# Expert weights of a mixture of experts: small load units for the first four experts, whole up matrices for the others, and the last down projection split by output columns

## What is computed

```
gate = one group of 4, top 2 of its 8 experts      # gate (n, 32), mostly zero
for e in range(32):                                # D_MODEL 1024, D_EXPERT 256
    hu = xt @ w_up[e]                              # (n,1024) @ (1024,512)
    h  = silu(hu[:, :256]) * hu[:, 256:]
    y += gate[:, e:e+1] * (h @ w_down[e])          # (n,256) @ (256,1024)
out = layernorm(ALPHA * x + y)
```

## Time and profile before

| | |
|---|---|
| time, median of 3 runs | 657.33 us (656.35 to 657.81) |
| the profiled execution | 656.87 us, its span 654.7 us |
| TensorE matmuls busy | 574.6 us, 88% of the span |
| VectorE, ScalarE, GpSimd busy | 297.1, 91.5, 42.8 us |
| moved by DMA | 163.51 MB, mean 250 GB/s |
| chain that ended last | TensorE 65%, VectorE 16%, DMA 15% |

### The profile page before, as it was taken

One profiled execution on the slowest core, in us unless ns is written; L12 is line 12 of the kernel. 1 busy time (PEld: TensorE's weight loads), 2 busy tenths in 40 slices (PEclk: granted clock), 3 DMA queues, 4 the chain that ended last, 5 costly groups with the idle time before them and its releaser, 6 DMA issues.

```text
span 654.7 us, 8625 instructions
## 1 busy us (share of the span) xinstructions
PE 574.6 (88%) x3514; PEld 362.4 (55%) x3514; DVE 297.1 (45%) x794; ACT 91.5 (14%) x215; POOL 42.8 (7%) x54
## 2 busy tenths in 40 slices
PE   6999999869999979999789996999999869778481
PEld 4556656556588757777566654875563424422130
DVE  1355675596765789788473386311001100100007
ACT  1001211014001232223100211011111101000010
POOL 0000000000100143223000000000000000000000
PEclk9999999995999989999899997799999979797896
DMA  8963044561244457564268645699999999999941
GB/s 301 374 247 128 2 162 187 184 195 49 67 128 132 125 182 235 139 218 140 88 257 343 231 209 226 239 394 407 419 366 419 420 419 419 421 418 420 420 189 68
DMA packets 47132, 163.51 MB, mean 250 GB/s; under 512 B 5842, under 2 KB 22700, under 8 KB 34420
## 3 DMA queue, kind: packets, MB, share of 16 engines
q1 hardware_dynamic: 38272, 138.78, 55.0%
q0 software_dynamic: 3472, 14.31, 6.4%
q10 hardware_dynamic: 5348, 9.86, 4.2%
HBM read 160.14 MB, written 2.77 MB: 249 GB/s over the span
## 4 chain that ended last, share of the span: by engine, by line
PE 65%; DVE 16%; DMA 15%; issue 2%; SPq 1%; ACT 0%; DVEq 0%
DMA ring<-in_w_up 13%; PE bank L665 12%; PE bank L494 10%; PE bank L939 6%; PE bank L456 4%; PE bank L926 4%; PE bank L784 4%; PE bank L908 4%; PE bank L1006 3%; PE bank L974 2%; PE bank L848 2%; PE bank L829 2%; PE bank L535 2%; PE bank L761 2%; DVE proj L1389 2%
## 5 line engine op out<-in xcount | busy, mean ns | idle before, releaser
L665 PE MATMUL bank<-work,ring 128*128 128x264 f32 x384 | 93.7, 397 | 0.0
L494 PE MATMUL bank<-ring,work 128*128 128x512 f32 (+2 forms) x224 | 90.5, 546 | 0.6 <-DMA ring<-in_w_in 0.6
L939 PE MATMUL bank<-ring,work 128*32 128x512 f32 x384 | 67.2, 672 | 19.6 <-DMA ring<-in_w_up 13.2
L665 PEld LDWEIGHTS bank<-work,ring 128*128 128x128 f32 x384 | 71.8, 193 | 16.0 <-issue 4.8
L494 PEld LDWEIGHTS bank<-ring,work 128*128 128x128 f32 x224 | 40.2, 190 | 31.0 <-issue 27.0
L2023 DVE SCALAR_TENSOR_TENSOR work<-work,bank 128x256 f32<-128x256 f32 x8 | 3.4, 422 | 100.9 <-ACT work L1276 100.9
L939 PEld LDWEIGHTS bank<-ring,work 128*32 128x32 f32 x384 | 18.4, 122 | 52.9 <-issue 52.8
L939 PE MATMUL bank<-proj,work 128*32 128x512 f32 x128 | 35.0, 697 | 10.4 <-DMA ring<-in_w_up 10.4
L926 PE MATMUL bank<-gates 128*128 128x256 f32 x144 | 36.6, 411 | 0.0
L2036 DVE COPY gates<-bank 128x512 f32<-128x512 f32 x8 | 5.5, 692 | 66.3 <-PE bank L1006 66.3
L926 PEld LDWEIGHTS bank<-gates 128*128 128x128 f32 x144 | 34.8, 335 | 0.5 <-issue 0.4
(11 more groups left out here) (305 smaller groups left out, 766.5 us busy)
## 6 DMA issues: line engine op xcount, KB each, us to landing
ring<-in_w_up SPq DMA_DIRECT2D x24, 2048.0 KB, 18.8
ring<-in_w_down SPq DMA_DIRECT2D x12, 2048.0 KB, 27.9
ring<-in_w_in SPq DMA_DIRECT2D x22, 1024.0 KB, 5.4
proj<-in_w_up SPq DMA_DIRECT2D x8, 2048.0 KB, 24.1
proj<-in_w_down SPq DMA_DIRECT2D x4, 2048.0 KB, 27.9
ring<-in_w_o SPq DMA_DIRECT2D x4, 1024.0 KB, 8.1
ring<-in_cache_mem_k ACTq DMA_DIRECT2D x1, 2048.0 KB, 7.8
ring<-in_cache_mem_v ACTq DMA_DIRECT2D x1, 2048.0 KB, 14.0
```

Of the source, the lines that this page charges most:

```text
L494: last = mm(bank[2 * (i % 2 if i < MEMC else 0) + t][:, 0:w], lhs[:, k, 128 * t:128 * t + 128], rhs[:, k % 4, :], start=(k == 0), stop=(k ...
L665: last = mm(b[:, 0:TOK], w[:, k, 128 * (n % 2):128 * (n % 2) + 128], xT[:, k, 0:TOK], start=(k == 0), stop=(k == KT - 1))
L939: last = mm(bank[5][32 * j:32 * j + 32, :], xTe[q // 2 % 2][:, k, s0:s0 + CAP], w2[j // 2][:, j % 2, r, :], start=(k == 0), stop=(k == KT ...
```

## The change

Quad 0 gets small units: an up unit holds rows k = 2u and 2u + 1 of all four experts (runs of 4 KB), a down unit one of the two rows f of all four (4 KB). TensorE takes them one at a time (`first_up`), between the gathers, and frees each when it is done.

Quads 1 to 7 get whole up matrices: an up unit is one expert, a run of 16 KB a partition. `up_rows` waits for expert j's unit at k = 0 and frees all four at k = 7. Down units are as before, apart from the first and the last quad.

The down units of the last quad hold all four experts for one half `dh` of the output columns (runs of 2 KB, two DMAs a unit). `down(7)` runs one half of the columns, frees its unit, then the other; ScalarE's copy waits only for the first. `combine_last(dh)` takes each half by itself, and VectorE's statistics are split in the same way (`y_part`). The same instructions are run as before, in another order.

```diff
             def expert_unit(w, u, e0):
-                d = wslot[w].rearrange("p (j n) -> p j n", j=2)
-                e = e0 + 2 * (u % 2)
                 if u < UPS:
-                    s = w_up[bass.ds(e, 2), :, :].rearrange("j (p r) n -> p j (r n)", p=128)
-                    at = 2048 * (u // 2)
+                    sp.dma_start(wslot[w], w_up[bass.ds(e0 + u, 1), :, :].rearrange("j (p r) n -> p (j r n)", p=128))\
+                        .then_inc(quad_in[w], 16)
                 else:
-                    s = w_dn[bass.ds(e, 2), :, :].rearrange("j (p r) n -> p j (r n)", p=128)
-                    at = 0
-                sp.dma_start(d, s[:, :, at:at + 2048]).then_inc(quad_in[w], 16)
+                    sp.dma_start(wslot[w].rearrange("p (j n) -> p j n", j=2),
+                                 w_dn[bass.ds(e0 + 2 * (u - UPS), 2), :, :].rearrange("j (p r) n -> p j (r n)", p=128))\
+                        .then_inc(quad_in[w], 16)
+            def row_unit(w, u):
+                d = wslot[w].rearrange("p (j n) -> p j n", j=4)
+                if u < UPS:
+                    s = w_up[0:4, :, :].rearrange("j (p r) n -> p j (r n)", p=128)
+                    at = 1024 * u
+                else:
+                    s = w_dn[0:4, :, :].rearrange("j (p r) n -> p j (r n)", p=128)
+                    at = 1024 * (u - UPS)
+                sp.dma_start(d, s[:, :, at:at + 1024]).then_inc(quad_in[w], 16)
+            def column_unit(w, dh):
+                d = wslot[w].rearrange("p (r j n) -> p r j n", r=2, j=4)
+                s = w_dn[NE - 4:NE, :, :].rearrange("j (p r) n -> p r j n", p=128)
+                for r in range(2):
+                    sp.dma_start(d[:, r, :, :], s[:, r, :, 512 * dh:512 * dh + 512]).then_inc(quad_in[w], 16)
...
-                expert_unit(w, n % WPQ, 4 * (n // WPQ))
+                if n < WPQ:
+                    row_unit(w, n)
+                elif n >= QUADS * WPQ - 2:
+                    column_unit(w, n - QUADS * WPQ + 2)
+                else:
+                    expert_unit(w, n % WPQ, 4 * (n // WPQ))
...
+            def up_rows(q, k0, k1):
+                n = WPQ * q
+                for k in range(k0, k1):
                     for j in range(4):
                         s0 = 4 * CAP * (q % 2) + CAP * j
+                        if k == 0:
+                            pe.wait_ge(quad_in[(n + j) % NWS], 16 * ((n + j) // NWS) + 16)
+                        last = mm(bank[5][32 * j:32 * j + 32, :], xTe[q // 2 % 2][:, k, s0:s0 + CAP],
+                                  wslot[(n + j) % NWS][:, 512 * k:512 * k + 512], start=(k == 0), stop=(k == KT - 1))
+                        if k == KT - 1:
+                            last.then_inc(used_w, 1)
+            def first_up(u):
+                w4 = wslot[u].rearrange("p (j r n) -> p j r n", j=4, r=2)
+                pe.wait_ge(quad_in[u], 16)
+                for r in range(2):
+                    k = 2 * u + r
+                    for j in range(4):
+                        last = mm(bank[5][32 * j:32 * j + 32, :], xTe[0][:, k, CAP * j:CAP * j + CAP], w4[:, j, r, :],
                                   start=(k == 0), stop=(k == KT - 1))
+                last.then_inc(used_w, 1)
...
+            def combine_last(dh):
+                pe.wait_ge((y_act, y_dve)[dh], QUADS)
+                pe.wait_ge(gt_sb, QUADS)
+                g_ = GT[(QUADS - 1) % 2]
+                for t in range(2):
+                    mm(bank[2 * t + dh][:, :], g_[:, 128 * t:128 * t + 128], Ysb[:, 512 * dh:512 * dh + 512],
+                       start=False, stop=True).then_inc(comb, 1)
+                for j in range(2 * dh, 2 * dh + 2):
+                    last = mm(bank[4][32 * j:32 * j + 32, 0:256], g_[:, 256:288], Ysb[:, 256 * j:256 * j + 256],
+                              start=False, stop=True)
+                if dh:
+                    last.then_inc(more_c, 1)
...
+                if q == 0:
+                    for f in range(2):
+                        w4 = wslot[n + f].rearrange("p (j d n) -> p j d n", j=4, d=2)
+                        pe.wait_ge(quad_in[n + f], 16)
+                        for dh in range(2):
+                            for j in range(4):
+                                last = mm(bank[6 + dh][32 * j:32 * j + 32, :], hT2[:, f, 32 * j:32 * j + 32],
+                                          w4[:, j, dh, :], start=(f == 0), stop=(f == 1))
+                        last.then_inc(used_w, 1)
+                    return
+                if q == QUADS - 1:
+                    for dh in range(2):
+                        w4 = wslot[(n + dh) % NWS].rearrange("p (f j n) -> p f j n", f=2, j=4)
+                        pe.wait_ge(quad_in[(n + dh) % NWS], 16 * ((n + dh) // NWS) + 32)
+                        for f in range(2):
+                            for j in range(4):
+                                last = mm(bank[6 + dh][32 * j:32 * j + 32, :], hT2[:, f, 32 * j:32 * j + 32],
+                                          w4[:, f, j, :], start=(f == 0), stop=(f == 1))
+                        last.then_inc(used_w, 1)
+                    return
...
+            first_gather(0, 0)
+            first_gather(0, 1)
             for i in range(4):
-                first_gather(0, i)
-            for b in range(2):
-                pe.wait_ge(first_sb, 2 * b + 2)
-                up_half(0, b)
+                pe.wait_ge(first_sb, i + 1)
+                first_up(i)
+                if i < 2:
+                    first_gather(0, i + 2)
...
-            combine(QUADS - 1)
+            combine_last(0)
+            combine_last(1)
...
-                act.wait_ge(used_w, WPQ * (q + 1))
+                act.wait_ge(used_w, WPQ * (q + 1) - (q == QUADS - 1))
...
+            def y_part(dh, t):
+                dve.wait_ge(comb, QUADS + 2 * dh + t)
+                link(V.bn_stats(stats[:, 12 * t + 6 * dh:12 * t + 6 * dh + 6], bank[2 * t + dh][:, :]))
...
+            y_part(0, 0)
+            y_part(0, 1)
+            y_part(1, 0)
             y_stats(0)
+            y_part(1, 1)
             y_stats(1)
```

More of the change, by code:

```diff
@@ L928, in gather @@
                     last.then_inc(gat_ps, 1)
[L930 to L936, removed]
+            def up_rows(q, k0, k1):
+                n = WPQ * q
+                for k in range(k0, k1):
                     for j in range(4):
                         s0 = 4 * CAP * (q % 2) + CAP * j
-                        last = mm(bank[5][32 * j:32 * j + 32, :], xTe[q // 2 % 2][:, k, s0:s0 + CAP], w2[j // 2][:, j % 2, r, :],
+                        if k == 0:
[11 more added lines that the diff above has]
+                        last = mm(bank[5][32 * j:32 * j + 32, :], xTe[0][:, k, CAP * j:CAP * j + CAP], w4[:, j, r, :],
                                   start=(k == 0), stop=(k == KT - 1))
-                        if r == 3 and j % 2 == 1:
-                            last.then_inc(used_w, 1)
+                last.then_inc(used_w, 1)
             def up(q):
@@ L947, in up @@
                     pe.wait_ge(gat_sb, 4 * (q // 2))
-                for b in range(2):
-                    up_half(q, b)
+                up_rows(q, 0, KT)
             def gate_turn(q):
@@ L970, in combine @@
                 g_ = GT[q % 2]
-                end = q == QUADS - 1
                 for t in range(2):
                     for dh in range(2):
[L974 to L977, removed]
+                        mm(bank[2 * t + dh][:, :], g_[:, 128 * t:128 * t + 128], Ysb[:, 512 * dh:512 * dh + 512],
+                           start=False, stop=False)
                 for j in range(4):
                     last = mm(bank[4][32 * j:32 * j + 32, 0:256], g_[:, 256:288], Ysb[:, 256 * j:256 * j + 256],
-                              start=False, stop=end)
-                last.then_inc(more_c if end else comb, 1)
+                              start=False, stop=False)
+                last.then_inc(comb, 1)
+            def combine_last(dh):
[3 more added lines that the diff above has]
+                for t in range(2):
+                    mm(bank[2 * t + dh][:, :], g_[:, 128 * t:128 * t + 128], Ysb[:, 512 * dh:512 * dh + 512],
+                       start=False, stop=True).then_inc(comb, 1)
[4 more added lines that the diff above has]
+                    last.then_inc(more_c, 1)
             def residual_in():
@@ L1053, in more @@
                 pe.wait_ge(more_xe, it + 1)
[L1054 to L1064, removed]
+                for k in range(KT):
+                    for j in range(4):
+                        if k == 0:
+                            pe.wait_ge(quad_in[RING6[j]], 16 * (QUADS * WPQ // NWS) + 16 * it + 16)
+                        last = mm(bank[5][32 * j:32 * j + 32, :], xTe[0][:, k, 32 * j:32 * j + 32],
+                                  wslot[RING6[j]][:, 512 * k:512 * k + 512], start=(k == 0), stop=(k == KT - 1))
+                        if k == KT - 1:
+                            last.then_inc(used_w, 1)
```

(6 more changed lines are left out.)

## The result

The changed kernel takes 659.92 us (median of 8 runs, 658.24 to 661.34) against 657.37 us (8 runs): ratio 1.0047, interval 1.0032 to 1.0063. It is slower by 2.6 us of medians, 3.1 us by the ratio (2.1 to 4.1); 0.6 us faster was forecast.

The account below looks back on a forecast made before the run. Bound: TensorE until down(1) ends at 477.4, then 28 units' transfers to 621.14, then a tail on TensorE and VectorE. 656.87 + 0.2 - 2.4 + 2.8 - 1.2 = 656.3, as a median 656.7 us; range 654.8 to 659.3.

Parts of the forecast that it names:

- up(7), foretold +2.8: Last quad's up: 58 MATMULs follow its last unit in place of 32; 26 more at 0.107 us cost 2.8 us.
- 58 MATMULs: In up(7): experts 0 to 2 multiply early at k = 0, so 29 of 32 multiplications follow the last unit.
- 16 KB runs, foretold -2.4: Up units of quads 1 to 7: longer runs shorten the transfers of 20 units by 2.4 us, lower bound 0.
- 1.9 to 3.0%: Time saved by 16 KB against 8 KB runs: 1.9% by rate delivered, 3.0% by engine share, of 99.6 us.
- The rival on the packet price: Saturated transfers: longer runs give only 0 to 0.6 us, time 658.5 to 659.1; chance 0.22, shared with the clock rival.
- Quad 0, foretold +0.2: Quad 0's small units: +0.2 us for the first_up that runs at half clock; bounds 0 and 0.5.
- the earlier issue is given back: Unit 8 goes out near 417.3, not 424.97, but transfers idle longer before down(1) ends, 3.5 us in place of 1.5.
- The last down, foretold -1.2: Last down, combine and VectorE statistics in halves: 5.44 us in place of 6.68, saving 1.2 us, between 0.9 and 1.5.
- The clock: TensorE idles some 12 us before up(7), regains full clock later, loses 1.3 us more: 658.0; chance within a shared 0.22.
- The cover against starving: Quads 1 to 7: later slot releases leave 7 us of cover, so transfers do not starve; rival within the 0.22.
- Unit 47: Last down unit, 2 KB runs: lands near 631, before down(7) at about 633; covered by 2 to 4 us.
- no gain, clock lost: Upper end of the whole range, 659.3 us: longer runs gain nothing and TensorE's clock comes back later.

Follow-up runs that it names:

- the part alone: The kernel before with whole up matrices in quads 1 to 7 alone, quad 0 and the last down as before: 660.22 us, ratio 1.0044.
- the loads alone: A kernel that only loads expert weights in groups by run length, no arithmetic: 422 GB/s at 8 KB, 429 at 16, 410 at 4, 387 at 2.
- the version with the small ones late: Kernel before with 16 KB units in quads 1-6, rows in quad 7, split, early count load, last combine's small multiplications together at its end: 652.46 us, ratio 0.9931.

## Why the prediction was wrong

The forecast had the four places right, and the two large effects in them: transfers that get shorter and work behind unit 45 that gets longer. Four sizes were off, all to the same side, 3.0 us in sum (-0.6 foretold, 2.4 by the stretches). In three of them a mechanism was wrong or missing, and not only a number: multiplications that run side by side, the price of alternating, and work of VectorE that nothing covers any more.

- **up(7), foretold +2.8, measured +3.6.** The failed step is "At 6.87/64 = 0.107 us each the 26 more are 2.8 us". A mean over instructions that run four abreast is no price of one. Nor do the early multiplications of experts 0 to 2 save anything, as "58 MATMULs" assumes. In steps it is 16 against 8 of 0.43 us, 3.4 us; the rest, 0.1 to 0.2, is the clock. Shown by the changed kernel with halves in quad 7 (3.4 us by the stretch) and by the part alone.
- **16 KB runs, foretold -2.4, measured -1.5.** "1.9 to 3.0%" was 1.6%: the upper end came from shares of busy time, which count the overlap of packets (2.1% by shares in the loads alone) and from 6 us beside another queue. The lower end set 428 GB/s, which is divided by the share, against 420, which is not. The loads alone gave 1.6%. This is the largest miss of the four, 0.9 us, though the mechanism stands. The rival on the packet price (0 to 0.6 us) did not come true: 1.5 of the 2.4 came.
- **Quad 0, foretold +0.2, measured +0.9.** I counted the same instructions and gave their order no price. The 0.2 stood for a first_up at half the clock, and that isn't what was paid: the full clock was back at about 416.6, when the first first_up began, and the first two took 1.85 us each. That the earlier issue is given back was right, and so was the place where.
- **The last down, foretold -1.2, measured -0.6.** Two small multiplications were priced at half of four, and the work under TensorE's combine (VectorE's load and branch) was not asked what covers it. The first is shown by the version with the small ones late; the second delayed the first statistic and cost 0.2 us at the end. Besides, the large ones of one half took 1.9 us and the next one 1.1, not 1.72 and 0.86: the mean of eight in a row is too small for groups of two.
- **The clock** was at half when unit 45 landed, before and after. up(7)'s 16 steps are 6.9 us at 2.4 GHz, so 1.9 us of 8.75 are its loss, against 1.8 before (5.19 less 3.44). The other quads' rows in the chain lose 1.8 to 2.9 us against the 6.31 of quad 3, which had the full clock. In four profiles with whole matrices in quad 7 the loss is 1.9 to 2.5 us (mean 2.1), in five with halves 1.6 to 2.6 (mean 1.9). So this rival is not needed for the 2.4 us of the two profiles; a later clock by 0.2 or 0.3 us in the mean is not excluded, 1.3 is.
- **The cover against starving** held: from 482 to 629 no stretch of 1 us has a DMA share under 0.79. **Unit 47** was in before down(7)'s second half, though with 2 KB runs the rate fell to 380 to 390 GB/s in stretches of 1 us.

The range (654.8 to 659.3) missed by 0.6 us. Its upper end is called "no gain, clock lost", but by the prediction's own terms that is 656.7 + 2.4 + 1.3 = 660.4: the end was set 1.1 us too low. A range up to 660.4 would have held the result by luck, since neither of its two terms came true. It had no term for up(7) and the last combine, whose prices I held for known.

## What to carry to other kernels

When the end hangs on the last load, cut that load so that the least work follows it, and along the dimension that all parallel tiles share: rows of all four experts leave 4 steps behind the last unit, halves 8, whole matrices 16 (3.6, 5.2 to 6.0 and 8.8 to 9.3 us here). In this kernel long runs paid where nothing waits on the last unit of a quad, and short ones at the end. And before a multiplication is priced by its count, look at the starts in the timeline: here tiles in different column groups started together (four MATMULs every 0.43 us), and halving their number saved nothing.

## What the runs showed of the hardware

In the kernel of loads alone a packet from HBM cost 9 to 10 ns beside its bytes from 2 KB to 16 KB runs (387, 410, 422 and 429 GB/s). A gather of 12 MATMULs with 128x128 weight loads took 3.06 us behind a group of 128x32 ones and 2.94 us in the mean of four in a row; the first projection took 14 or 16 us on the same instructions from one profile to another, at a granted clock of 1.00 both times, and why stays open.
